# Sample value products of a hybrid decoder trunk in twelve visits of two

## The reference, cut to what matters

```python
h = rms_norm(x, g_norm) @ w_in                 # 1024 -> 8192 columns, split among the branches
# A: differential attention, 4 heads, values 128 wide, cache paged (2 pages of 128 tokens)
# B: dilated windows (128,1), (512,4), (2048,16), 4 heads of 64
# M: cross-attention into 256 memory tokens, 4 heads of 64
o_a = diff_attend(...); o_b = dilated_combine(groups); o_m = memory_attend(...)
mixed = g0 * ((o_a*silu(za)) @ w_proj_a) + g1 * ((o_b*silu(zb)) @ w_proj_b) + g2 * ((o_m*silu(zm)) @ w_proj_m)
y = rms_norm(x + mixed @ w_out, g_final)
```

## Time and profile before

| | us |
|---|---|
| median of 3 runs (lowest, highest) | 639.76 (639.39, 644.63) |
| the profiled execution, its own time | 640.16 |
| its span in the profile | 638.5 |
| TensorE busy / VectorE / ScalarE / GpSimd | 618.2 / 327.8 / 284.9 / 101.7 |
| B and M attention, slots 2 to 26 | about 324.4 to 427.7 |

### The profile page before, as it was taken

The page is one execution under the profiler, slowest core; times in us unless marked ns, Lnnn a source line. Parts: engine busy times, 40 slices in busy tenths (PEclk is TensorE's granted clock), DMA queues, the critical chain, the costliest instruction groups (busy, mean ns, idle before and its releaser), DMA issues.

```text
span 638.5 us, 12050 instructions
## 1 busy us (share of the span) xinstructions
PE 618.2 (97%) x4899; PEld 567.4 (89%) x4899; DVE 327.8 (51%) x682; ACT 284.9 (45%) x572; POOL 101.7 (16%) x184
## 2 busy tenths in 40 slices
PE   7999999899999999999999999999999999999996
PEld 5999999788999999999988776669999999998774
DVE  3953113866525956646574645445828237146134
ACT  6754344565556234335555545447443332322131
POOL 2200100000013314657414312200000000010000
PEclk8899999989999999999999999999999999999999
DMA  8426533210237855776522435221352433242003
GB/s 292 143 87 211 174 125 101 67 52 17 67 117 227 286 181 180 245 228 200 162 61 74 146 100 182 81 82 45 111 164 70 151 112 108 93 148 85 1 2 132
DMA packets 58441, 81.54 MB, mean 128 GB/s; under 512 B 4601, under 2 KB 48177, under 8 KB 58130
## 3 DMA queue, kind: packets, MB, share of 16 engines
q1 hardware_dynamic: 49538, 54.54, 26.4%
q0 software_dynamic: 8848, 26.23, 13.2%
HBM read 73.51 MB, written 7.24 MB: 126 GB/s over the span
## 4 chain that ended last, share of the span: by engine, by line
PE 87%; DVE 5%; DMA 3%; ACT 2%; issue 1%; POOL 0%; SPq 0%; DVEq 0%; ACTq 0%; POOLq 0%
PE pj L769 19%; PE pj L770 18%; PE pj L771 18%; PE pt_bank L882 3%; PE ps L769 2%; PE ps L770 2%; PE ps L771 2%; PE ps L780 2%; PE po_bank L919 1%; PE ps L831 1%; PE ps L861 1%; PE pj L1012 1%; DVE w_lo L1523 1%; DMA out<-stage 1%; PE ps L1142 1%
## 5 line engine op out<-in xcount | busy, mean ns | idle before, releaser
L769 PE MATMUL pj<-xh,w_hi 128*128 128x260 f32 x1024 | 294.9, 288 | 0.0
L770 PE MATMUL pj<-xh,w_lo 128*128 128x260 f32 x1024 | 289.9, 283 | 0.0
L771 PE MATMUL pj<-xl,w_hi 128*128 128x260 f32 x1024 | 289.7, 283 | 0.0
L769 PEld LDWEIGHTS pj<-xh,w_hi 128*128 128x128 f32 x1024 | 193.5, 189 | 9.1 <-issue 8.0
L770 PEld LDWEIGHTS pj<-xh,w_lo 128*128 128x128 f32 x1024 | 193.6, 189 | 0.2
L771 PEld LDWEIGHTS pj<-xl,w_hi 128*128 128x128 f32 x1024 | 193.7, 189 | 0.0
L1523 DVE TENSOR_TENSOR w_lo<-w_raw,w_hi 128x1024 fp32r<-128x1024 f32 x78 | 92.9, 1221 | 137.5 <-ACT w_hi L1176 137.5
L1176 ACT ACTIVATE w_hi<-w_raw 128x1024 fp32r<-128x1024 f32 x78 | 79.0, 1049 | 2.5 <-POOL w_raw L620 2.5
L1239 ACT ACTIVATE region<-pj 128x260 f32<-128x260 f32 x44 | 17.0, 386 | 68.8 <-PE pj L771 68.6
L1239 ACT ACTIVATE gate<-pj 128x260 f32<-128x260 f32 x44 | 17.0, 387 | 66.4 <-PE pj L771 66.4
L769 PE MATMUL ps<-oh,w_hi 128*128 128x260 f32 x96 | 27.4, 285 | 0.7 <-DVE ol L1890 0.3
(11 more groups left out here) (340 smaller groups left out, 994.3 us busy)
## 6 DMA issues: line engine op xcount, KB each, us to landing
w_raw<-in_w_in SPq DMA_DIRECT2D x64, 512.0 KB, 4.3
ring<-in_cache_diff_kv POOLq DMA_DIRECT2D x32, 256.0 KB, 3.5
out<-stage SPq DMA_DIRECT2D x19, 256.0 KB
ring<-in_cache_mem_kv POOLq DMA_DIRECT2D x16, 256.0 KB, 3.7
w_raw<-in_w_out SPq DMA_DIRECT2D x8, 512.0 KB, 4.8
w_raw<-in_w_mem_kv SPq DMA_DIRECT2D x4, 512.0 KB, 8.1
region<-in_x_prompt SPq DMA_DIRECT2D x4, 512.0 KB, 10.3
q_all<-q_rows POOLq DMA_DIRECT2D x8, 256.0 KB, 3.9
```

What stands on the lines that cost most here:

```text
L769: pe.matmul(out, wh, mh, start=(i == 0), stop=False)
L770: pe.matmul(out, wl, mh, start=False, stop=False)
L771: last = pe.matmul(out, wh, ml, start=False, stop=(i == n - 1))
```

## The change

The order of the value loads becomes A 0, M 0, A 1, M 1, up to A 7, M 7, and then B 0 to 7. The products are done in twelve visits, each with two neighbouring entries of the list: slots 4, 6, 8, 10, 12, 14, 16 and 18 do A and M of one sample, slots 19, 21, 23 and 25 do B of two samples. A visit waits for both loads before its first matmul. The two places of `ring`, the wait of load k for product k - 2, and the matmuls themselves stay as they are.

```diff
-        RINGS += [(k, b) for k in "BAM" for b in range(NS)]
+        RINGS += [(k, b) for b in range(NS) for k in "AM"] + [("B", b) for b in range(NS)]
+        VISITS = {s: NK + 2 * i for i, s in enumerate([4, 6, 8, 10, 12, 14, 16, 18, 19, 21, 23, 25])}
...
-                    if sample_first:
-                        sample_values(NK + s - a - 3)
+                    if sample_first and s - a in VISITS:
+                        two_samples(VISITS[s - a])
                     if a <= s - 3:
                         values(s - 3)
-                    if which == "BM" and s >= a + 3 and not sample_first:
-                        sample_values(NK + s - a - 3)
+                    if which == "BM" and s - a in VISITS and not sample_first:
+                        two_samples(VISITS[s - a])
...
-            def sample_values(k):
-
-                kind, b = RINGS[k]
-                pe.wait_ge(s_kr[k % 2], KR[k])
+            def two_samples(k):
+
+                for i in (k, k + 1):
+                    pe.wait_ge(s_kr[i % 2], KR[i])
                 if k == NK:
                     pe.wait_ge(s_sev, 3)
+                for i in (k, k + 1):
+                    sample_values(i)
+
+            def sample_values(k):
+
+                kind, b = RINGS[k]
                 slot = ring[:, k % 2, :, :]
```

More of the change, by code:

```diff
@@ L998, in samples_probs_b @@
                 pe.matmul(out[0:80, 128:160], e_b[:, 128:208], g_b, start=True, stop=True).then_inc(s_saT, 1)
+            def two_samples(k):
+                for i in (k, k + 1):
+                    pe.wait_ge(s_kr[i % 2], KR[i])
+                if k == NK:
+                    pe.wait_ge(s_sev, 3)
+                for i in (k, k + 1):
+                    sample_values(i)
             def sample_values(k):
                 kind, b = RINGS[k]
-                pe.wait_ge(s_kr[k % 2], KR[k])
-                if k == NK:
-                    pe.wait_ge(s_sev, 3)
                 slot = ring[:, k % 2, :, :]
```

## The result

The changed kernel is slower. Its ratio to the kernel before is 1.0069 (95% interval 1.0042 to 1.0095), some 4.4 us; the median of its nine runs is 646.4 us, outside the range of 637.5 to 643.7. The nine runs of the kernel before beside them have a median of 640.0, so the medians lie 6.4 us apart; the means, 645.8 and 641.2, lie 4.6 apart, near to what the ratio gives. What follows explains the 4.4. The profiled execution took 644.59 us around a span of 642.9. The work moved as forecast, but the low clock behind the stall, the late loads of M and a small loss of cover cost more than in the sum.

A forecast was written before the change was run, and what follows sets the result against it. TensorE's own order of work was taken to bound the kernel (87% of the chain). Products -5.30, stall +4.05 and low clock +1.5 sum to +0.25 us on 639.76: 640.0 us, no change, range 637.5 to 643.7.

The forecast's parts named there:

- The product terms: Sample visits in slots 3 to 26: -2.00, -3.92 and +0.62, together -5.30 us.
- The stall: Slot 19's visit waits for B 0 and B 1 after slot 18's: 4.05 us, between 3.85 and 4.75.
- I take 1.5: Lower clock once behind slot 19's stall, as for 3.4 us after 127.8: a loss of 1.5 us, bounds 0 and 5.1.
- The rival of the long lower clock: Behind slot 19's stall the clock stays low as in the opening, losing 5.1 us, not 1.5: 643.6 us, chance 0.18.
- The agreement that the prediction saw at 127.8 us: The clock fell to 1.2 GHz from 127.8 to 131.2 us after a 1.88 us wait, taken as matching the skill's rule.
- holds at the median with 0.5 to spare: Slots 14 to 16: M's load lands after 7.05 us, at most 8.45, within 7.58; costed at nothing, 0 to 1 in range.
- Slot 3's visit was to give 0.56: Slots 3 to 10: each of four odd slots loses its B visit, 0.56 us each, 2.24 us less.
- I had costed VectorE and ScalarE at nothing: Shorter slots leave these engines less time; TensorE would not wait more: 0, bounds 0 to 0.4 us in all.
- Its base: Time of the kernel before, taken as the median of its runs: 639.76 us.
- that the clock holds: Rival: the clock stays full through slot 19's stall, -5.30 + 4.05 = -1.25, 638.5 us; chance 0.15.
- that M does not run beside A: Rival: each of eight A and M visits costs up to 0.56 us more, 4.5 in all: 644.5 us; chance 0.06.
- that the loads are in time: Rival: no stall at slot 19, so -5.30 us: 634.5 us; chance 0.04.

The follow-up runs named there:

- the kernel with early visits and early reads: Changed kernel with visits in slots 2 to 18 even, 21, 23, 25 and page numbers read before the ring wait: 634.4 us, repeats 637.5 and 636.3.
- the kernel before again: The kernel before, unchanged, run once more: 641.6 us, ratio 1.0005.
- the two other profiles with an open stall: Changed kernel with page numbers read before the ring wait (ratio 1.0027), and changed kernel with its first two value loads issued late (ratio 1.0043).
- filling the stall: Changed kernel plus 16 f32 matmuls on ones in slot 19 ahead of the visit: 643.9 us, ratio 1.0032; with early page reads too, 641.3 us.
- late first loads: Changed kernel with only the first two value loads issued after the last rows are turned: 644.7 us, ratio 1.0043.
- early page reads: Changed kernel with GpSimd reading both page numbers of an A load before its wait for the ring place: 644.3 us, ratio 1.0027.

## Why the prediction was wrong

**The product terms held, and gave a little more.** At equal clock at the start of the stage, the kernel with early visits and early reads takes 110.4 us where the kernel before again takes 115.6: 5.2 less, with 0.9 of late loads inside, 6.1 without. The forecast was 5.3 for the changed kernel; by the same terms this one gains 5.2 too (slot 2 pays 0.98 more, slot 19 is freed). From slot 4 to 18 the changed kernel gave 4.77 with 1.32 us of late M loads inside, 6.1 without, where I had 5.4. Part of that is that a visit ahead of a unit costs more than its own 0.98: transposes and unit together take 3.59 us to the next transposes after (371.35 to 374.94), against 0.81 + 2.99 in the earlier trace rows.

**The stall held.** 3.94 us against 4.05, and the visit of slot 19 after 6.22 us against 6.25.

**The clock was mis-sized: the first step that failed.** The step "I take 1.5", from one low stretch of 3.4 us, was too small. The clock was low for 6.8 us here and for 10.2 in the two other profiles with an open stall, and that costs 2.7, 3.4 and 3.6 us by filling the stall (2.0 and 2.4 by the ratios). Its place was right, and so was the price of a microsecond of it: 2.7 us for 6.8, 0.4 each, against 1.5 for 3.4. The length was wrong, because it came from a single row. Behind the same wait for ScalarE at about 124 us, 1.9 us long in every profile, the clock was low for 3.4 us in six of the 17 profiles, for 6.8 in one and not at all in ten. The rival of the long lower clock put it down to the waits and short products behind the stall; that these set the length isn't shown, for the same instructions at the start of the stage met 3.4 us of low clock in one profile of the changed order and 6.8 in another.

The Trainium skill (TensorE: Matmul & The Clock Gate, section "HAM oscillation — how this bites in real kernels") says that an engine that waits for transfers between bursts is throttled and begins the next one cold. The trace agrees at slot 19 (lower clock from 401.9 us on, behind 3.94 us of wait for a transfer). The agreement that the prediction saw at 127.8 us was of another kind, since that wait was for ScalarE.

**The reloads were costed at nothing: the second step that failed.** The step was "holds at the median with 0.5 to spare": a landing of 3.1 us after an issue at 3.95. In the profile after, M's transfer was issued 4.26 us after the visit in slot 4 (336.17 to 340.43), and the seven M transfers up to 400 us landed as follows, against the earlier trace rows before:

```profile
340.43 0.72 POOL L657 DMA_DIRECT2D ring<-in_cache_mem_kv  x1
```

```profile
DMA to landing us min/median/max: 3.5/3.7/4.9
```

A median of transfers that mostly run alone was taken for transfers that follow two others. Of the eight M transfers in the earlier trace rows one stood behind two A transfers, the one issued at 392.80 that gave the 3.95. The kernel before has for it alone:

```profile
DMA to landing us min/median/max: 4.5/4.5/4.5
```

So the row of the very situation was the one that the prediction took for the worst case. The other seven had 3.0 to 3.7 us. The late loads cost 1.3 us in this profile, and 1.6 and 1.9 in the profiles with late first loads and with the stall filled. The 2.7 us between the ratios with and without early page reads isn't their price: the intervals overlap, and 0.8 us of waits stayed. And the shortest distance was not the only place. The wait in slot 16 stands at it, but slot 10 had 0.9 us more (362.06 - 0.64 - 353.04 = 8.38 against 386.78 - 0.68 - 378.67 = 7.43 from slot 14 to 16) and waited 0.64: its M transfer took 4.9 us, the longest of the seven, beside two weight loads of 512 KB, with the transfer engines 94% busy from 358 to 362 us, where 340 to 344 had 56%.

**A cover was gone in slot 4.** Slot 3's visit was to give 0.56. With a low start in both, first scores to slot 4's visit took 19.18 us; the kernel before again, with slot 3's visit in it, needs 0.1 more (316.25 to 335.54), where 0.56 was forecast. The timeline of the changed kernel shows where it went:

```profile
332.86 1.31 PE L832 MATMUL ps<-region 64*128 64x128 f32 x8 [0.19 <-DVE small L1656]
...
335.15 1.10 PE L902 MATMUL po_bank<-work,v_b 128*64 128x128 f32 x24 [0.25 <-ACT work L1304]
```

I had costed VectorE and ScalarE at nothing, with 0.4 as the bound; these two waits come to 0.44.

**The sum, mended:** -5.3 - 0.7 + 0.4 + 3.9 + 2.7 + 1.3 = 2.3 us with this profile's numbers, against 0.25 forecast and 2.6 measured in the stage at equal start. To the 4.4 us of the ratio some 2 us stay open, with an interval of 1.7 us on either side of it. Part of it is that the profiled execution was a mild one. With the means of three profiles each for the clock (3.2) and for the late loads (1.6) the sum is 3.1, an estimate, and 1.3 us stay open. Candidates are late loads that weigh more in other executions than in the profiled ones (with early visits the early reads gain 3.4 to 6.0 us by the ratios, where the waits for M in the profiles fall by 2.8), and the longer wait ahead of the first scores, for which no run gave a price. The range failed with this: I had added late M loads of at most 1 us and a short clock to it, and never summed a long lower clock with late loads. Its base was low too: 639.76, the median of three runs, where 119 later executions of the kernel before have a median of 641.5.

The rivals: that the clock holds falls, that M does not run beside A falls (20 ns apart), that the loads are in time falls. The case on the other side, the long lower clock, was the nearest, with 643.6, and it still lay below the 646.4.

## What to carry to other kernels

Two products in one visit free both places of a double buffer at once: the distance to the next visit must then hold the issue of all transfers one behind another plus a landing under that load, so look at the smallest distance in the loop, not the usual one, and at the visits beside which other transfers run. Here one pair of neighbouring slots and late page reads turned a gain of some 0.8% into a loss of 0.7%. Moving the pair apart takes the ratio from 1.0069 to 0.9979; with the page numbers read ahead of the wait too, the same idea beats the kernel before (ratios 0.9886, 0.9926 and 0.9908). Price a stall of TensorE as its length plus the low clock behind it, and take the length of that from several profiles: a single row can be 0, 3.4 or 6.8 us for the same instructions. And take a landing time from transfers that are queued as yours will be, even if there is only one such row.

## What the runs showed of the hardware

Eight f32 matmul records on four groups of 32 output partitions, with 512 columns of one tile on two groups and 256 of another on the other two, take 0.99 us, as four with 512 columns on two groups do (0.98). The lower clock came at about 318 us, after waits of 0.7 to 3.1 us and small products, in 14 of 17 profiles, of kernels old and new: 2.7 us of difference between two profiles of one program. A stall of 3.9 us was followed by it in three profiles of three, and in none of two when it was filled. An M transfer of 256 KB landed 3.0 to 3.7 us after its issue with none of A's ahead of it, in the kernel before, and 3.5 to 4.9 behind two of A's, in the changed kernel; with early visits and early reads 3.6 to 6.1. And 119 executions of the kernel before, unchanged, lay between 638.8 and 647.3 us, the slower the lower their mean granted clock (correlation -0.8), so less than about 2 us cannot be read from a few runs of it.
